# A hybrid decoder layer on one core: other work leads on ScalarE, GpSimd and TensorE at four places of the mixer

## The reference

```python
def _decoder_layer(x, ...):
    x = _layer_norm(DN_ALPHA * x + 0.5 * _swiglu(x, f1g, f1u, f1d), ln_g[0], ln_b[0])
    m, s_new, new_k, new_v = _mixer(x, w_in, w_out, gn_w, sinks, ret_state, k_buf, v_buf)
    x = _layer_norm(DN_ALPHA * x + m, ln_g[1], ln_b[1])
    x = _layer_norm(DN_ALPHA * x + 0.5 * _swiglu(x, f2g, f2u, f2d), ln_g[2], ln_b[2])

def _mixer(h, ...):
    rq, rk, rv, rg, sq, sk, sv = _project_in(h, w_in)
    o_ret, s_new = _retention(rq, rk, rv, s0, RET_CHUNK)   # state S' = g*S + k^T v; o = scores*mask @ v + q S
    o_swa = _swa_prompt(sq, sk, sv, sinks)                 # window 128, ALiBi, sinks; decode over a cache
    y_ret = silu(rg) * _head_group_norm(o_ret, gn_w)       # per head of 64: subtract mean, divide by deviation
    merged = concatenate([y_ret, o_swa], axis=-1)
    return merged @ w_out, s_new, new_k, new_v
```

## Time and profile before

| | |
|---|---|
| median of 3 runs | 2163.05 us (2161.7 to 2163.13) |
| profiled execution, its own time | 2158.6 us |
| its span, first to last instruction | 2156.8 us |
| mean granted TensorE clock | 0.989 |
| busy: PE / DVE / ACT / POOL | 98% / 42% / 24% / 24% |

### The profile page before, as it was taken

How to read it: one execution, slowest core, us unless ns; L and a number is a source line. 1 busy time by engine, 2 the same in 40 slices (tenths; PEclk the granted TensorE clock), 3 DMA queues, 4 the chain that set the end, 5 groups by cost and what they waited for, 6 DMA issues and landing times.

```text
span 2156.8 us, 31091 instructions
## 1 busy us (share of the span) xinstructions
PE 2104.2 (98%) x11989; PEld 1933.1 (90%) x11989; DVE 911.2 (42%) x1690; ACT 507.1 (24%) x887; POOL 514.3 (24%) x257
## 2 busy tenths in 40 slices
PE   8999999999999999999988999999999999999997
PEld 8999999999999979999786667999999999999996
DVE  5535353535353462102545636343434343434346
ACT  4111112121112162111135444312121212121115
POOL 3221212121212132222352223212121212121213
PEclk9999999999999999999899999999999999999999
DMA  7010111111010112111114011110101010101012
GB/s 285 30 58 30 58 36 52 46 42 56 32 58 30 40 51 91 40 39 42 55 58 155 1 42 42 59 59 29 58 29 58 29 58 29 58 29 58 29 59 84
DMA packets 38074, 118.40 MB, mean 55 GB/s; under 512 B 6271, under 2 KB 10879, under 8 KB 37759
## 3 DMA queue, kind: packets, MB, share of 16 engines
q1 hardware_dynamic: 38015, 117.58, 15.4%
HBM read 106.29 MB, written 11.27 MB: 55 GB/s over the span
## 4 chain that ended last, share of the span: by engine, by line
PE 94%; DVE 2%; issue 1%; ACT 1%; DMA 1%; POOL 1%; SPq 0%; DVEq 0%; ACTq 0%
PE bank L119 20%; PE bank L121 20%; PE bank L120 20%; PE bank L460 7%; PE bank L459 7%; PE bank L461 7%; PE bank L1854 2%; PE bank L1856 2%; PE bank L1855 2%; PE bank L1824 1%; PE bank L457 1%; PE bank L456 1%; PE bank L1774 1%; PE bank L751 1%; PE bank L1795 1%
## 5 line engine op out<-in xcount | busy, mean ns | idle before, releaser
L119 PE MATMUL bank<-x_hi,f_w_hi 128*128 128x362 f32 (+1 forms) x2104 | 689.1, 328 | 0.5 <-DVE x_low L162 0.5
L121 PE MATMUL bank<-x_hi,f_w_low 128*128 128x362 f32 (+1 forms) x2104 | 689.0, 327 | 0.0
L375 POOL TENSOR_TENSOR f_w_low<-f_w_raw,f_w_hi 128x1024 fp32r<-128x1024 f32 x132 | 316.6, 2413 | 1182.4 <-ACT f_w_hi L293 1182.3
L561 DVE TENSOR_TENSOR acc<-bank,acc 128x512 f32<-128x512 f32 x720 | 468.0, 686 | 7.8 <-PE bank L461 4.4
L539 DVE TENSOR_TENSOR f_h_full<-bank,f_silu 128x362 f32<-128x362 f32 (+1 forms) x132 | 70.6, 535 | 813.9 <-PE bank L121 811.7
L119 PEld LDWEIGHTS bank<-x_hi,f_w_hi 128*128 128x128 f32 x2104 | 395.9, 188 | 2.6 <-issue 0.8
L121 PEld LDWEIGHTS bank<-x_hi,f_w_low 128*128 128x128 f32 x2104 | 396.1, 188 | 0.0
L120 PE MATMUL bank<-x_lo,f_w_hi 128*128 128x362 f32 (+1 forms) x1056 | 345.4, 327 | 0.0
L120 PE MATMUL bank<-x_low,f_w_hi 128*128 128x362 f32 (+1 forms) x1048 | 342.8, 327 | 0.0
L461 PE MATMUL bank<-f_w_low,f_h_hi 128*128 128x512 f32 x640 | 250.3, 391 | 0.0
L460 PE MATMUL bank<-f_w_hi,f_h_lo 128*128 128x512 f32 x640 | 250.2, 391 | 0.0
(11 more groups left out here) (206 smaller groups left out, 2224.2 us busy)
## 6 DMA issues: line engine op xcount, KB each, us to landing
f_w_raw<-ffn_in SPq DMA_DIRECT2D x132, 512.0 KB, 4.4
rp_w_raw<-w_ret_in SPq DMA_DIRECT2D x16, 512.0 KB, 3.5
acc<-x_rows_in SPq DMA_DIRECT2D x2, 2048.0 KB, 11.1
kept_rows<-acc SPq DMA_DIRECT2D x8, 512.0 KB, 2.8
ow_raw<-w_out_in SPq DMA_DIRECT2D x8, 512.0 KB, 6.8
y_out<-acc SPq DMA_DIRECT2D x8, 512.0 KB, 2.7
n_rows<-ln_rows_in SPq DMA_DIRECT2D x6, 512.0 KB, 5.3
gp_stage<-w_att_in SPq DMA_DIRECT2D x4, 512.0 KB, 3.5
```

The costliest lines, as they stand in the source:

```text
L119: pe.matmul(out, wh, xh, start=first, stop=False)
L121: return pe.matmul(out, wl, xh, start=False, stop=last)
L375: pool.tensor_tensor(flat(w_lo[s][j]), flat(w_raw[s][j]), flat(w_hi[s][j]).bitcast(F32), ALU.subtract).then_inc(done, 1)
L561: dve.tensor_tensor(acc[:, t, d], down_ps[(n + 2 * s) % 4][:, :], acc[:, t, d], ALU.add).then_inc(down_free, 1)
```

## The change

1. `FIRST` is a list by hand: Q and K of chunks 0 and 1 lead, then V and GATE of these chunks, then chunk 2.
2. The decode states and outputs of retention go pair by pair: states 0, outputs 0, states 1, outputs 1, a projection, states 2, outputs 2, states 3, outputs 3. DVE waits pair by pair; ACT copies the outputs when all four pairs are done. ACT copies block 7's output before, not after, it rounds the first weight tile of the next stage. (Two semaphores for cleared memory become one.)
3. In the group norm ACT does `high(j-3)` before `square(j)` and `deviation(j)`, and GpSimd does `low(j-3)` before `normalise(j)`.
4. In attention ACT does in step i the exponentials of item i+3, not i+4 (those of item 4 move behind step 0), and the low parts of the four odd w_out tiles go from DVE to GpSimd, in its order behind the scaling of items 5, 6, 7 and 9.

```diff
-    FIRST = [(c, j) for c in range(len(CHUNKS)) for j in range(4)]
+    FIRST = [(0, Q), (0, K), (1, Q), (1, K), (0, V), (0, GATE), (1, V), (1, GATE), (2, Q), (2, K), (2, V), (2, GATE)]
...
-            copy_k(0, c, 4 + 4 * c + K + 1)
+            copy_k(0, c, 4 + FIRST.index((c, K)) + 1)
...
-    def last_outputs(pe):
+    def last_outputs(pe, t):
         a, b, w = tokens(LAST)
-        pe.wait_ge(masked, 2 * LAST + 2)
-        pe.wait_ge(zeroed, 1)
-        pe.wait_ge(out_read, LAST)
-        pe.wait_ge(dec_in, 16)
-        pe.wait_ge(q_ready, LAST + 1)
-        for t in range(PAIRS):
+        if t == 0:
+            pe.wait_ge(masked, 2 * LAST + 2)
+            pe.wait_ge(zeroed, 2)
+            pe.wait_ge(out_read, LAST)
+            pe.wait_ge(dec_in, 16)
+            pe.wait_ge(q_ready, LAST + 1)
...
         if t < 2:
-            pe.wait_ge(state_done, BLOCKS)
+            pe.wait_ge(state_done, BLOCKS - 1 + t)
...
-        dve.wait_ge(out_done, LAST + 1)
         for t in range(PAIRS):
+            dve.wait_ge(out_done, LAST + t + 1)
             dve.wait_ge(kv_done, BLOCKS + t + 1)
...
-        act.wait_ge(out_done, LAST + 1)
+        act.wait_ge(out_done, LAST + PAIRS)
...
-        retention.last_outputs(pe)
         retention.last_states(pe, 0)
+        retention.last_outputs(pe, 0)
         retention.last_states(pe, 1)
+        retention.last_outputs(pe, 1)
         project(0)
         retention.last_states(pe, 2)
+        retention.last_outputs(pe, 2)
         retention.last_states(pe, 3)
+        retention.last_outputs(pe, 3)
         pe.wait_ge(*retention.outputs_read)
...
         for j in range(STEPS):
+            if 0 <= j - 3 < TOKEN_TILES - 1:
+                high(j - 3)
             if j < TOKEN_TILES:
                 square(j)
                 deviation(j)
-            if 0 <= j - 3 < TOKEN_TILES - 1:
-                high(j - 3)
...
         for j in range(STEPS):
+            if 0 <= j - 3 < TOKEN_TILES - 1:
+                low(j - 3)
             if j < TOKEN_TILES:
                 normalise(j)
-            if 0 <= j - 3 < TOKEN_TILES - 1:
-                low(j - 3)
...
-    def split(self, dve, k):
+    def split_even(self, dve, k):
         dve.wait_ge(self.hi_done, k + 1)
...
+    def split_odd(self, pool, k):
+        pool.wait_ge(self.hi_done, k + 1)
+        pool.tensor_tensor(self.low[k][:, :], self.raw[k][:, :], self.hi[k][:, :].bitcast(F32),
+                           ALU.subtract).then_inc(self.odd_lo_done, 1)
...
-                    pe.wait_ge(out_weights.lo_done, k + 1)
+                    pe.wait_ge(out_weights.odd_lo_done if k % 2 else out_weights.even_lo_done, k // 2 + 1)
...
             for k in ROUNDED_AT.get(i - 1, ()):
-                out_weights.split(dve, k)
+                if k % 2 == 0:
+                    out_weights.split_even(dve, k)
...
-            if i + SLOTS < LAST:
-                exponentials(act, i + SLOTS)
+            if 0 < i < LAST - SLOTS + 1:
+                exponentials(act, i + SLOTS - 1)
...
+            for k in ROUNDED_AT.get(i - SLOTS, ()):
+                if k % 2:
+                    out_weights.split_odd(pool, k)
...
             retention.scalar(act)
+            retention.scalar_second(act)
             gp.scalar_early(act, 0)
-            retention.scalar_second(act)
```

More of the change, by code:

```diff
@@ L1197, in tensor @@
             output(n)
-    def last_outputs(pe):
+    def last_outputs(pe, t):
         a, b, w = tokens(LAST)
-        pe.wait_ge(masked, 2 * LAST + 2)
-        pe.wait_ge(zeroed, 1)
-        pe.wait_ge(out_read, LAST)
-        pe.wait_ge(dec_in, 16)
-        pe.wait_ge(q_ready, LAST + 1)
-        for t in range(PAIRS):
-            for h in range(2):
-                pe.matmul(out_ps[h][HD * h:HD * h + HD, w * t:w * t + w], v_tok[:, LAST, head(t, h)],
-                          probs[LAST % 2][:, h, w * t:w * t + w], start=True, stop=False)
-            for s in range(DEC_BATCH):
-                i = slice(DEC_SEQ * s, DEC_SEQ * s + DEC_SEQ)
-                for h in range(2):
-                    d = slice(HD * h, HD * h + HD)
-                    mm = pe.matmul(out_ps[h][d, w * t + i.start:w * t + i.stop],
-                                   state_dec[d, t, s, :], q_dec[LAST % 2][d, t, i],
-                                   start=False, stop=s == DEC_BATCH - 1)
+        if t == 0:
[4 more added lines that the diff above has]
+            pe.wait_ge(q_ready, LAST + 1)
+        for h in range(2):
+            pe.matmul(out_ps[h][HD * h:HD * h + HD, w * t:w * t + w], v_tok[:, LAST, head(t, h)],
+                      probs[LAST % 2][:, h, w * t:w * t + w], start=True, stop=False)
+        for s in range(DEC_BATCH):
+            i = slice(DEC_SEQ * s, DEC_SEQ * s + DEC_SEQ)
+            for h in range(2):
+                d = slice(HD * h, HD * h + HD)
+                mm = pe.matmul(out_ps[h][d, w * t + i.start:w * t + i.stop],
+                               state_dec[d, t, s, :], q_dec[LAST % 2][d, t, i],
+                               start=False, stop=s == DEC_BATCH - 1)
         mm.then_inc(out_done, 1)
@@ L1232, in vector @@
         dve.memset(state[0][:, :, :], 0.0)
-        dve.memset(state[1][:, :, :], 0.0).then_inc(cleared, 1)
+        dve.memset(state[1][:, :, :], 0.0).then_inc(zeroed, 1)
         dve.wait_ge(mask_in, 16)
@@ L1255, in vector @@
             if n == 0:
-                dve.wait_ge(cleared, 1)
+                dve.wait_ge(zeroed, 1)
             else:
@@ L1627, in __init__ @@
         self.staged = [core.semaphore(f"ow_staged{k}") for k in range(KT // 2)]
-        self.hi_done, self.lo_done = core.semaphore("ow_hi_done"), core.semaphore("ow_lo_done")
+        self.hi_done = core.semaphore("ow_hi_done")
+        self.even_lo_done, self.odd_lo_done = core.semaphore("ow_even_lo_done"), core.semaphore("ow_odd_lo_done")
     def load(self, sp, k):
```

6 lines of the change are left out of this document (3 added, 3 removed).

## The result

| | before | after |
|---|---|---|
| median, us | 2162.38 (4 runs, 2160.98 to 2163.13) | 2142.82 (4 runs, 2141.93 to 2146.34) |
| profiled execution's own time; its span | 2158.6; 2156.8 | 2143.15; 2141.3 |
| mean granted clock | 0.989 | 0.994 |
| TensorE's waits (span less busy time) | 52.6 | 44.9 |

The ratio is 0.9913, with a 95% interval of 0.9896 to 0.9931: 19.6 us faster by the medians, where 18.3 were predicted (2144.8 us, measured 2142.82). The interval stands for 14.9 to 22.5 us, so it can't tell the forecast from one a few us off. The spans of the two profiled executions differ by 15.5 only: the profiled execution of before (2158.6) was faster than all four runs of its median.

A forecast was written before the change was run, and what follows sets the result against it. TensorE was busy for 98% of the span, so only its 52.6 us of waits and the half-clock stretches beside them could be won. Terms 0 + 8.5 + 4.8 + 5.0 = 18.3 us, from 2163.05 to 2144.8 us; range 2138 to 2154.

The forecast's parts named there:

- FIRST, 0: Start of the retention projection: the new list moves only products nobody waited for, so 0 us, give or take a few tenths.
- Group norm, 8.5: End of the group norm: TensorE's 7.2 us of waits go, and 1.3 us of half clock behind them; bounds 7.2 and 8.8.
- With `low` ahead of `normalise` the loop is cut: Group norm: GpSimd's reordering alone ends the three-engine loop in which DVE sat 14.8 us waiting for the low part.
- End of retention, 4.8: Block 7's output to the turning of tile 0: 4.8 us won, two thirds of the way between 0.2 and 7.1.
- The full-clock case (13.9 us): End of retention: the stretch of 21.1 us takes 13.9 us if the clock stays full, 7.1 us won.
- a clock of 0.50 for 13 us: Sign that the forecast is wrong: half clock for 13 us behind retention.
- the fall came behind the 1.89 us gap: End of retention: argument for full clock, that the clock fell after TensorE's 1.89 us wait for ACT's copy.
- The added wait for ACT: End of retention: before the turning of tile 0 TensorE waits for ACT to empty banks, 0.77 us and 0.2 for releases.
- Start of attention, 5.0: Start of attention: later exponentials spare ACT its waits for DVE's maxima, so ACT sets the pace; 5.0 us won, between 0 and 8.
- the free value of 6.2: Start of attention: the gain of 6.2 us if DVE and GpSimd do not disturb each other.
- Half clock and collisions: Rival, chance 0.22: half clock stays through the decode outputs (0.2 won), GpSimd's pieces collide every step (2 won); 10.7 us, 2152.3.
- The slower case: Rival, chance 0.04: attention's output waits in every step, costing 24 us, more than the 18.3 won; 2169 us.

The follow-up runs named there:

- i1_project_last: The changed kernel with the first projection behind all four pairs of decode states and outputs, not between the second and third: 2144.79 us, against 2146.34 for the changed kernel.
- e4_attention: The changed kernel with one line undone, ACT's copy of block 7's output again behind the first weight rounding: 2146.95 us, ratio 0.9931 to the kernel before.
- i2_tile7: The changed kernel with the low part of w_out tile 7 back on DVE: 2139.61 us, against 2146.34 for the changed kernel beside it.

## Why the prediction was right, and where not

The time, the range and the sign held, and so did three of the four terms' causes. By its own steps:

- **FIRST, 0.** Right: -0.1 us. The wait at L751 stayed (2.2 us).
- **Group norm, 8.5.** Right in the result: 10.8 alone (7.8 to 13.6), 9.2 in its stretch. But the step "With `low` ahead of `normalise` the loop is cut" is wrong: that edit alone gave 1.6. I had booked ACT's `high` ahead of `square` as a cost of 0.6 us, where it was the other half of the cut. The rows showed it: GpSimd waited only 0.7 us for `mix_hi` because it came late itself, which said nothing of how early the rounding was. `back` no longer waits at all and the half clock behind the waits is gone, as said.
- **End of retention, 4.8.** Alone 4.0, between its bounds. The full-clock case (13.9 us) nearly came true for the stretch itself, 14.4 us, and "a clock of 0.50 for 13 us" did not come. What the step missed is where the rest of the half clock goes: into the turnings and the next projection. The added wait for ACT was sized right (0.87 us measured, 1 said). And "the fall came behind the 1.89 us gap" was no sign that the gap was the cause: i1_project_last has the fall with no gap. The Trainium skill (TensorE: Matmul & The Clock Gate, "Why this matters for your kernels") advises against long idle gaps of TensorE between bursts of matmuls. It does not account for the falls here: 10.2 us at 0.50 came behind a wait of only 0.6 us (e4_attention), and 13.8 us with no wait at all (i1_project_last).
- **Start of attention, 5.0.** Alone 3.3 by the medians (1.3 to 5.2) and 2.9 in c, in the whole kernel 3.5 to 4.0 (c). The mechanism was right: ACT waits 3.7 us for the first w_out load, hardly for the maxima, and the unit stops inside for tile 7, at 1188.6 to 1191.4. The mis-sized term is the disturbance. I took a loss of 1.2 us off the free value of 6.2; it was 2.2 to 2.7 (c of the changed kernel). The changed kernel's GpSimd pieces took 2.7 us and not 2.4, its scalings 2.2 and not 1.9, DVE's pieces 1.75. And I costed tile 7's move as the place where the sum ends, without asking what it would be on DVE: 2.2 to 2.7 us less (i2_tile7), and without the fall of the clock that one of the two profiles has behind the wait.
- **The rivals.** "Half clock and collisions" was too dark: of the 13.6 us of half clock 6.8 stayed, and attention won 3.5 to 4.0 where that rival gave it 2. The slower case had no sign of it; TensorE's 87.7 us after the first unit are full but for the 2.8 us.
- **Slips in the working.** Two low parts that end 3.43 us after 1182.92, if the first began only at 1184.13, take 1.11 us each and not 1.15. With the clock as low for as long, 13.9 + 6.8 ends 0.4 us earlier and not 0.2. Neither moves the forecast.

That the sum came out so close is in part luck. By the medians of the parts two errors cancel, 2.3 us too little for the group norm, 0.8 and 1.7 too much for the other two, though the interval of each takes in its term; and the second comparison of the same kernel gave 15.5 us where the first gave 19.6.

## What to carry to other kernels

When engines wait on each other in a ring, list every instruction in each engine's queue that stands ahead of the late one and itself waits for the ring: one that is left can hold up the whole ring, and a first cut that gives a sixth of the gain doesn't refute the second. Put a last piece that everybody waits for on the engine that can start it first, not on the one with more idle time. And read how busy time itself changes for the same instructions: half of what this change won between the two profiles was clock, in part kept by one wide projection between small products with no wait ahead of them.

## What the runs showed of the hardware

That 0.6 us of TensorE's waiting is followed by 10.2 us of half clock (e4_attention, one profile), and that the clock can fall with TensorE busy without a break (i1_project_last), was not expected.

Nor was how long a tiny operation can take. In the changed kernel, DVE's timeline, then GpSimd's:

```profile
1178.54 1.61 DVE L1917 TENSOR_TENSOR at_stats<-at_stats,small 128x4 f32<-128x4 f32 x1
1180.19 0.16 DVE L1919 TENSOR_TENSOR at_stats<-small,at_stats 128x4 f32<-128x4 f32 x1
```

```profile
1177.78 2.35 POOL L1648 TENSOR_TENSOR ow_low<-ow_raw,ow_hi 128x1024 fp32r<-128x1024 f32 x1
```

L1917 works on four columns, as L1919 does in 0.16 us. It took 1.61 and ended at 1180.15, with GpSimd's piece, which ended at 1180.13. The rule that the prediction took from the Trainium skill (SBUF — State Buffer, "Who interferes with whom") covers it, two SBUF inputs on DVE beside a GpSimd read; what the run adds is that four columns waited for GpSimd's whole piece, and they are of the maxima that ACT's next exponentials wait for.
